# An opening in long rows with products of zeros, and splits of weights moved behind nearer work, in a one-layer hybrid encoder kernel

## The reference

```python
h = rmsnorm(x, g_norm1); z = h @ w_in
rq, rk, rv, rg, fq, fk, fv, ff, mq, gl = jnp.split(z, SPLIT_POINTS, axis=-1)
mk, mv = jnp.split(rmsnorm(mem, g_mem_in) @ w_mem_kv, 2, axis=-1)   # 256 memory tokens
# o_r: retention; o_f: forgetting attention; o_m: attention into the memory tokens
merged = (gates[..., 0, :] * (o_r @ w_br_ret)
          + gates[..., 1, :] * (o_f @ w_br_fox)
          + gates[..., 2, :] * (o_m @ w_br_mem))
x = x + merged @ w_out
return x + hier_moe(rmsnorm(x, g_norm2), ...)   # top-1 of 4 groups, top-2 of 8 experts in it
```

## Time and profile before

| | us |
|---|---|
| median of 3 runs (lowest to highest) | 654.72 (654.51 to 655.26) |
| the profiled execution | 654.53 |
| its span, first to last instruction | 652.6 |
| PE busy in it | 630.6 |
| DVE busy | 341.8 |
| ACT busy | 255.9 |
| POOL busy | 126.8 |

### The profile page before, as it was taken

How to read it: one execution, slowest core, us unless ns; L and a number is a source line. 1 busy time by engine, 2 the same in 40 slices (tenths; PEclk the granted TensorE clock), 3 DMA queues, 4 the chain that set the end, 5 groups by cost and what they waited for, 6 DMA issues and landing times.

```text
span 652.6 us, 9424 instructions
## 1 busy us (share of the span) xinstructions
PE 630.6 (97%) x3509; PEld 422.7 (65%) x3509; DVE 341.8 (52%) x729; ACT 255.9 (39%) x489; POOL 126.8 (19%) x142
## 2 busy tenths in 40 slices
PE   5999999999999999999999999999999999999995
PEld 4888888877888776778777878764434444344431
DVE  4649347885456565754446855575433434334312
ACT  5673343336424555564953334332221212221200
POOL 0018525663000310010000010012301311210301
PEclk9999999999999999999999999999999999999999
DMA  8975432354212833203967989399999999999993
GB/s 307 421 278 193 152 128 101 113 211 169 97 66 97 298 130 130 98 33 130 341 214 294 428 321 372 138 411 351 428 424 425 427 427 425 425 427 426 426 420 122
DMA packets 36096, 176.67 MB, mean 271 GB/s; under 512 B 4256, under 2 KB 4528, under 8 KB 23632
## 3 DMA queue, kind: packets, MB, share of 16 engines
q1 hardware_dynamic: 33072, 164.87, 64.0%
q0 software_dynamic: 2976, 11.16, 4.8%
HBM read 167.48 MB, written 9.06 MB: 270 GB/s over the span
## 4 chain that ended last, share of the span: by engine, by line
PE 80%; SPq 5%; DMA 5%; ACT 5%; issue 2%; DVE 2%; POOLq 0%; ACTq 0%; POOL 0%; DVEq 0%
PE banks L1718 15%; PE banks L1720 15%; PE banks L1719 15%; PE banks L2101 12%; PE banks L2131 6%; SPq L835 5%; DMA piece<-in_wexp 4%; PE banks L2085 2%; PE banks L2141 1%; DMA raw<-in_wstream 1%; ACT z L1140 1%; PE banks L1926 1%; ACT w_hi L1020 1%; PE banks L2006 1%; PE banks L1892 1%
## 5 line engine op out<-in xcount | busy, mean ns | idle before, releaser
L1263 DVE TENSOR_TENSOR w_lo<-raw,w_hi 128x1024 fp32r<-128x1024 f32 (+1 forms) x81 | 125.0, 1554 | 75.0 <-ACT w_hi L1020 74.8
L1718 PE MATMUL banks<-w_hi,hT_hi 128*128 128x512 f32 x312 | 124.6, 399 | 1.0 <-ACT z L1047 0.9
L1720 PE MATMUL banks<-w_hi,hT_lo 128*128 128x512 f32 x312 | 122.0, 391 | 0.0
L1719 PE MATMUL banks<-w_lo,hT_hi 128*128 128x512 f32 x312 | 121.7, 390 | 0.0
L1020 ACT ACTIVATE w_hi<-raw 128x1024 fp32r<-128x1024 f32 x79 | 83.5, 1057 | 90.1 <-PE banks L1720 86.1
L2101 PE MATMUL banks<-piece,xs 128*64 128x512 f32 x512 | 114.7, 593 | 0.5 <-DMA piece<-in_wexp 0.5
L2101 PEld LDWEIGHTS banks<-piece,xs 128*64 128x64 f32 x512 | 38.5, 137 | 72.6 <-issue 70.1
L1718 PEld LDWEIGHTS banks<-w_hi,hT_hi 128*128 128x128 f32 x312 | 58.7, 188 | 13.5 <-issue 2.1
L1720 PEld LDWEIGHTS banks<-w_hi,hT_lo 128*128 128x128 f32 x312 | 58.6, 188 | 12.6
L1719 PEld LDWEIGHTS banks<-w_lo,hT_hi 128*128 128x128 f32 x312 | 58.8, 188 | 11.3
L2131 PE MATMUL banks<-piece,act_T 128*64 128x512 f32 x256 | 58.5, 599 | 0.1
(11 more groups left out here) (358 smaller groups left out, 949.9 us busy)
## 6 DMA issues: line engine op xcount, KB each, us to landing
piece<-in_wexp SPq DMA_DIRECT2D x90, 1024.0 KB, 18.5
raw<-in_wstream SPq DMA_DIRECT2D x79, 512.0 KB, 4.6
piece<-in_wexp SPq DMA_DIRECT2D x12, 512.0 KB, 20.6
foxc<-in_foxc POOLq DMA_DIRECT2D x8, 512.0 KB, 4.9
memv<-in_memc SPq DMA_DIRECT2D x8, 512.0 KB, 4.9
memk<-in_memc SPq DMA_DIRECT2D x8, 512.0 KB, 5.1
xT<-in_xT SPq DMA_DIRECT2D x1, 1536.0 KB, 11.5
xtok<-in_xtok SPq DMA_DIRECT2D x1, 1536.0 KB, 7.9
```

The lines of the kernel that those rows point to most:

```text
L1263: dve.tensor_tensor(w_lo[:, i % PART_SLOTS, cols], raw[:, i % RAW_SLOTS, cols], w_hi[:, i % PART_SLOTS, cols].bitcast(F32), ALU.subtract). ...
L1718: mm(out, xh, wh, start=start, stop=False, skip_group_check=True)
L1719: mm(out, xh, wl, start=False, stop=False, skip_group_check=True)
L1720: return mm(out, xl, wh, start=False, stop=stop, skip_group_check=True)
```

## The change

- **Opening.** The gains of the first two norms and the first half of the transposed memory are packed on the host into one array `opening` (rows of 1040 floats), loaded in one transfer. Granule 0 comes whole, then granule 1, then the rest of the memory, then granules 2 and 3. `xT` follows granule 5 instead of granule 3, and `prep_x` moves from behind granules 1 to 3 to behind granules 4 to 6. `gk` keeps only the gain of the last norm and is loaded at granule 4. Granule 1, like 0, is split in halves.
- **Products of zeros.** Before its first step PE does 26 products of 128x256 of a tile that POOL sets to zero at the start, into bank 7, which nothing reads. Of granule 0 the first two products (high by high) wait only for the high parts.
- **Splits.** The split of 13 moves ahead of the evacuations of chunks 0 and 1; those of 37 to 40 move behind the next group of turns (37 behind the evacuation of chunk 8 and five turns, 38 behind seven, 39 behind eight, 40 behind `decay_sums`); those of 63 and 65 move behind the merges of chunks 15 and 16. In those places `granule(g, 1)` leaves one split ahead in front of the granule, and `splits(n)` adds those up to n later.
- **Granules.** 51, with the evacuation of chunk 12, moves ahead of the transposes and softmax steps of the unit there. 66 and 67 move into the end of the attention, each cut in two slices. 73 is cut in two around `turn_merged 1`.
- **SP.** Pieces 0, 1 and 2 are loaded together when the attention is done; before, 0 was, and 1 and 2 followed at granules 66 and 67.

```diff
@@ schedule
-    prep = {1: [("prep_x", k) for k in range(3)], 2: [("prep_x", k) for k in range(3, 6)], 3: [("prep_x", 6), ("prep_x", 7), ("prep_ff",)], 9: [("norm1",)]}
+    prep = {4: [("prep_x", k) for k in range(3)], 5: [("prep_x", k) for k in range(3, 6)], 6: [("prep_x", 6), ("prep_x", 7), ("prep_ff",)], 9: [("norm1",)]}
...
+    def granule(g, ahead=ahead):
+        splits(g + 1 + ahead)
         s.append(("k", g))
         s.extend(prep.get(g, []))
...
-            granule(g)
+            granule(g, 1 if g == FIRST[C_GATE] - 1 else ahead)
             if g == FIRST[C_RQK] + 2:
+                s.append(("split", split))
+                split += 1
                 s += [("evac", C_MK), ("post", C_MK), ("evac", C_MV), ("post", C_MV)]
...
         if i in (4, 11, 19):
-            gate()
+            gate(1)
...
         opened(i)
+        if j == 3:
+            gate()
         turned(i - 2, True)
...
-    granule(r + 1)
+    granule(r + 1, 1)
     merge(r + 1)
+    splits(r + 4)
...
-    granule(r + 3)
+    granule(r + 3, 1)
     merge(r + 3)
+    splits(r + 6)
...
-    s += [("unit_o", n + 1), ("unit_p", n + 2), ("unit_v", n + 2), ("unit_p", n + 3), ("unit_o", n + 2), ("unit_v", n + 3), ("unit_o", n + 3)]
-    s += [("attention_done",)] + [("parts", j) for j in range(8, 12)]
+    s += [("unit_o", n + 1), ("unit_p", n + 2)]
+    granule(r + 6)
+    s += [("unit_v", n + 2), ("unit_p", n + 3), ("k2", r + 6), ("unit_o", n + 2), ("unit_v", n + 3)]
+    granule(r + 7)
+    s += [("unit_o", n + 3), ("attention_done",), ("k2", r + 7)] + [("parts", j) for j in range(8, 12)]
     c = C_BR + 4
-    granule(FIRST[c] - 2)
-    granule(FIRST[c] - 1)
...
-    s.append(("turn_merged", 1))
+    s += [("turn_merged", 1), ("k2", a + 1)]
@@ SP
-            load(gk, io["gk"], s_memT[0])
-            load(memT[:, 0:2, :], io["memT"][:, 0:2, :], s_memT[0])
-            load(raw[:, 0, 0:512], io["wstream"][0, :, 0:512], raw_in[0])
-            load(raw[:, 0, 512:1024], io["wstream"][0, :, 512:1024], second_half_in)
-            load(memT[:, 2:8, :], io["memT"][:, 2:8, :], s_memT[1])
-            for g in range(1, RAW_SLOTS):
+            load(opening[:, 0:2 * KT + KT // 2 * NMEM], io["opening"], s_memT[0])
+            granule(0)
+            granule(1)
+            load(memT[:, 4:8, :], io["memT"], s_memT[1])
+            for g in range(2, RAW_SLOTS):
                 granule(g)
-            load(xT[:, :, :], io["xT"], s_xT_ffw)
-            load(ffw, io["ffw"], s_xT_ffw)
@@ PE
+            pe.wait_ge(zeros_and_new, 1)
+            for _ in range(26):
+                mm(ps[:, 7, 0:256], nf_p[:, 0:P], nf_p[:, :], start=True, stop=True, skip_group_check=True)
...
+                    if i == 0:
+                        pe.wait_ge(act_hi, 2)
+                        pe.wait_ge(hi_ready, 1)
+                        for t in range(nt):
+                            mm(ps[:, bank_of(0, t), :], memT_hi[:, 0, t * P:t * P + P], w_hi[:, 0, 0:512], start=True, stop=False, skip_group_check=True)
```

More of the change, by code:

```diff
@@ L91, in schedule, with splits @@
     split = ahead + 1
-    prep = {1: [("prep_x", k) for k in range(3)], 2: [("prep_x", k) for k in range(3, 6)], 3: [("prep_x", 6), ("prep_x", 7), ("prep_ff",)], 9: [("norm1",)]}
-    def granule(g):
+    prep = {4: [("prep_x", k) for k in range(3)], 5: [("prep_x", k) for k in range(3, 6)], 6: [("prep_x", 6), ("prep_x", 7), ("prep_ff",)], 9: [("norm1",)]}
+    def splits(n):
         nonlocal split
-        while split < min(g + 1 + ahead, NGRAN):
+        while split < min(n, NGRAN):
             s.append(("split", split))
             split += 1
+    def granule(g, ahead=ahead):
+        splits(g + 1 + ahead)
         s.append(("k", g))
@@ L123, in schedule, with gate @@
     gates = iter(range(FIRST[C_GATE], FIRST[C_BR]))
-    def gate(evacs=s):
+    def gate(ahead=ahead):
         g = next(gates)
-        granule(g)
+        granule(g, ahead)
         if g + 1 in FIRST:
-            evacs.append(("evac", chunk_at[g]))
+            s.append(("evac", chunk_at[g]))
     chunk_at = [c for c in range(len(CHUNKS)) for _ in range(FIRST[c], FIRST[c + 1])]
@@ L400, in program @@
         ident = cst("ident")
[L401 removed]
+        gk = sm(KT)
         ss, rstd = sm(5), sm(5)
@@ L922, in _ @@
                     sp.wait_ge(br_add, 3)
-                    load_piece(0)
+                    for c in range(3):
+                        load_piece(c)
                 elif kind == "residual" and i == 0:
@@ L1016, in _ @@
                         act.activation(w_hi[:, 0, 0:512], raw[:, 0, 0:512], ACT.Copy).then_inc(hi_ready, 1)
-                        act.wait_ge(second_half_in, 16)
                         act.activation(w_hi[:, 0, 512:1024], raw[:, 0, 512:1024], ACT.Copy).then_inc(hi_ready, 1)
+                    elif i == 1:
+                        for half in range(2):
+                            cols = slice(512 * half, 512 * half + 512)
+                            act.activation(w_hi[:, 1, cols], raw[:, 1, cols], ACT.Copy).then_inc(hi_ready, 1)
                     else:
@@ L1259, in _ @@
                         dve.wait_ge(gran_used, i - PART_SLOTS + 1)
-                    for half in range(2) if i == 0 else (None,):
-                        dve.wait_ge(hi_ready, 1 if half == 0 else i + 2)
+                    for half in range(2) if i < 2 else (None,):
+                        dve.wait_ge(hi_ready, low_of(i) - (half == 0))
                         cols = slice(0, 1024) if half is None else slice(512 * half, 512 * half + 512)
@@ L1774, in _ @@
                             w = i % PART_SLOTS
-                            ins = parts(acc, xh[:, j, tok], xl[:, j, tok], w_hi[:, w, cols], w_lo[:, w, cols], first, last)
+                            if i == 0 and kk == 0:
+                                mm(acc, xh[:, j, tok], w_lo[:, w, cols], start=False, stop=False, skip_group_check=True)
+                                ins = mm(acc, xl[:, j, tok], w_hi[:, w, cols], start=False, stop=last, skip_group_check=True)
+                            else:
+                                ins = parts(acc, xh[:, j, tok], xl[:, j, tok], w_hi[:, w, cols], w_lo[:, w, cols], first, last)
                             if what == "out" and last and t < 2:
@@ L2276 @@
     arrays = {
-        "xT": turned(x), "xtok": by_token(x, T), "memT": turned(mem), "memtok": by_token(mem, 2), "gk": c(gk), "gain": c(np.tile(gain, (P, 1))),
+        "xT": turned(x), "xtok": by_token(x, T), "memT": c(memT[:, 4:]), "memtok": by_token(mem, 2), "gk": c(by_feature[2]),
+        "opening": c(np.concatenate(by_feature[:2] + [memT[:, :4].reshape(P, -1)], axis=1)), "gain": c(np.tile(gain, (P, 1))),
         "const": const, "const2": const2, "dtab": dtab, "qtab": qtab, "ffw": c(wff.reshape(KT, P, 8).transpose(1, 0, 2).reshape(P, 64)),
```

66 lines of the change are left out of this document (37 added, 29 removed).

## The result

| us | before | after |
|---|---|---|
| median of four runs (lowest to highest) | 654.65 (654.51 to 655.26) | 649.36 (648.57 to 649.76) |
| the profiled execution | 654.53 | 649.76 |
| its span | 652.6 | 648.0 |

The ratio is 0.9916, 95% interval 0.9904 to 0.9928: 5.3 us faster, where 5.4 was forecast (649.3). One thing to keep in mind: the profiled execution of the changed kernel is the slowest of the four.

A forecast was written before the change was run, and what follows sets the result against it. The end of the dense part starts PE and the piece stream together, so gains before granule 79 move the end. 1.8 + 0.7 + 0.35 + 0.45 + 1.3 + 0.85 = 5.45 us won, forecast 649.3 us, range 646.8 to 652.2.

The forecast's parts named there:

- The two rivals that rested on the stream of pieces: Expert part: the stream holds the end at 654.7 (chance 0.07); or PE waits for a piece, clock falls, 656.9 (0.04).
- Opening: Start of the kernel: 1.8 us won, bounds -0.3 and 2.3, with granule 3 at 16.4 against 18.29.
- the transfers cost a part of it: Opening: 0.26 MB more cost 0.78 us, less 0.40 for `gk`, so ACT begins granule 0 at 6.9, not 6.54.
- the gain comes from the clock: Opening: products of zeros raise the clock at 5.5, so products of weights start 0.23 us apart instead of 0.44.
- the clock is not won: Opening: zeros do not raise the clock earlier, or it falls, or granule 0 lands later; 650.8; chance 0.20.
- The idle 1.5 us: Opening: PE idles from the end of the products of zeros at 6.2 until the first real product at 7.7.
- The bound from granule 9's landing: Opening: granule 9 is split only from 31.18, when its data lands, so no more than 2.3 us can be kept.
- Turns 0.7: Six-fold transposes: splits moved behind the turns take away most of a 0.87 us stall; 0.7 won, bounds 0 and 1.0.
- granule 51 0.35: Granule 51 with the evacuation of chunk 12: transposes lie in front during ACT's copies; 0.35 us won, bounds 0 and 0.9.
- merges: Merges of chunks 15 and 16: 0.45 us won, bounds 0 and 1.9; the rest is waited for at `pT`.
- 73: Granule 73 around `turn_merged 1`: the 0.66 us stall before granule 74 goes; 0.85 won, bounds 0 and 1.0.
- Attention's end 1.3: Granules 66 and 67 in the end of the attention: their slices fill PE's gaps; 1.3 us won, bounds 0 and 1.7.

The follow-up runs named there:

- numbers 1: The changed kernel run again with no edit: 648.99 us (648.25 to 651.70), ratio 0.992.
- 7: The changed kernel with granules 66 and 67 put behind the attention again: 649.08 us.
- Number 8: The changed kernel with granule 65 also cut in two slices around transposes, and the values step in front of granule 66: 647.81 us, ratio 0.9897.
- Number 2: The changed kernel without the 26 products of zeros: 649.38 us (649.10 to 649.62).
- 3: The changed kernel with the load of `xtok`, `gain` and `gk` one step later, behind granule 9: 648.01 us, ratio 0.9896.
- 4: The changed kernel with `xtok` loaded behind granule 9 and no products of zeros: 649.24 us.
- Number 5: The kernel before with the 26 products of zeros alone: 654.95 us, ratio 1.0011; run once more, 656.33 us, ratio 1.0019.
- 11: The changed kernel with `xtok` loaded behind granule 9 and 14 products of zeros instead of 26: 648.99 us.
- number 10: The changed kernel with `xtok` behind granule 9, the edit of Number 8, and the split of 65 behind the transposes of unit 32: 646.62 us, ratio 0.9875.

## Why the prediction was right, and where its steps were not

**What bounds the kernel: right.** The end of granule 79, the first piece and the end of the span moved by 4.60, 4.60 and 4.69. In every run from the end of granule 79 to the end of the span it was 236.8 to 237.4 us. The two rivals that rested on the stream of pieces found nothing.

**The total: partly luck.** The stages behind the opening gave 3.2 where 3.65 was forecast: 1.0 too little at the attention's end, 0.6 more than forecast elsewhere. The opening, forecast at 1.8, gave 1.4 in the first profile and 2.3 to 3.0 in those of numbers 1, 7 and 8. That these came to 5.3 against 5.4 in the medians of four executions is not to the credit of the sum.

**Opening: the size was 1.8, the runs give 1.4 to 3.0; two of its steps failed.** The first was "the transfers cost a part of it". They gained. The 0.26 MB more did not move granule 0's split from 6.54 to 6.9; it started at 5.82 in the first profile, and at 5.4 to 5.5 in those of numbers 1 to 4. Granule 1, split from 10.27 before, is split from 8.06. The issue view shows it, before and after:

```profile
memT<-in_memT SPq DMA_DIRECT2D x1, 256.0 KB, 3.9
```

```profile
opening<-in_opening SPq DMA_DIRECT2D x1, 520.0 KB, 3.3
```

Twice the bytes landed 0.6 us sooner after their issue, and 1.05 us earlier in the span (by ACT's first rows, 4.08 against 5.13). The windows of 1 us show when the data began to flow:

```profile
1.00:2.00 1.00, 0.00 (x0) 0.00 (x0) 0.00 (x0) 1.00 (x1) 0.04 (x1) 1.00 0.10 12
2.00:3.00 1.00, 0.00 (x0) 0.00 (x0) 0.00 (x0) 0.01 (x1) 0.00 (x0) 1.00 0.35 111
3.00:4.00 1.00, 0.00 (x0) 0.00 (x0) 0.00 (x0) 0.00 (x0) 0.00 (x0) 1.00 0.74 225
4.00:5.00 1.00, 0.00 (x0) 0.00 (x0) 0.00 (x0) 0.00 (x0) 0.00 (x0) 1.00 1.05 283
```

```profile
1.00:2.00 1.00, 0.90 (x4) 0.90 (x5) 0.00 (x0) 1.00 (x1) 0.04 (x1) 1.00 0.30 62
2.00:3.00 1.00, 1.00 (x7) 1.00 (x7) 0.00 (x0) 0.02 (x1) 0.00 (x0) 1.00 0.86 320
3.00:4.00 1.00, 1.00 (x6) 1.00 (x6) 0.00 (x0) 0.00 (x0) 0.00 (x0) 1.00 1.00 383
4.00:5.00 1.00, 1.00 (x7) 1.00 (x6) 0.37 (x1) 0.91 (x2) 0.00 (x0) 1.00 1.33 340
```

From 1 to 5 us this is 0.63 MB before and 1.11 MB now. My 330 GB/s were of a window in which the stream was running; before, it started late. I counted bytes at a steady rate where the cost was in getting going. Whether it was the small rows of `gk`, the number of transfers or the length of their rows was not tried apart. The Trainium skill, "DMA: Bandwidth & Descriptors", section "Anatomy of one DMA — SWDGE (gpsimd) path", would have said 2.0 + 0.53 MB at 436 GB/s = 3.2 us for `opening`; the trace has 3.3, though SP issued it. I set that aside because the first piece before took 3.9 where it gives 2.6, but that was the second transfer of a queue, and `opening` is the first. By that fit the prediction had `opening` and granule 0 there at about 5.6, nearer to the 5.4 to 5.8 of the runs than my 6.9. The handoff to PE, which I had put at 0.15 without a row, was 0.15 in the first profile (5.82 + 0.63 to 6.60).

The second was "the gain comes from the clock". Number 5 has the clock without the transfers: nothing. Number 2 has the transfers without the zeros: 1.9 of the 2.6 us at granule 10. Both together are needed for the whole. In the kernel before, the landing of granule 1 covered the slow products; once it lands earlier, they are the bound, and only then are zeros worth something (1.2 to 1.6). For the same reason the rival "the clock is not won" had its price wrong: without any zeros the kernel took 649.38, not 650.8. The idle 1.5 us between the zeros and the first product of weights did not come about: the zeros ran up to it, at 6.60.

The bound from granule 9's landing (2.3 at most) was the right place to look: in the first profile it cut 2.40 to 1.39, and wherever PE waited there, the first product came 2.5 us after ACT began the split (32.05 and 34.58, 30.72 and 33.26, 31.13 and 33.66). But I took 31.18 for a constant, though the change moves `xT` behind two granules, and ACT's start varied between 30.4 and 32.1. In three of the five profiles with this opening more than 2.3 was kept at granule 9 (2.5 to 3.0).

**Turns 0.7, granule 51 0.35, merges 0.45, 73 0.85: right in mechanism**, measured 0.77, 0.52, 0.68, 0.95. The merges went as described: 1.49 was won at granule 62, and at granule 65 0.65 of it was left, the rest waited for at `pT`. The turns' two thirds and the 0.35 for granule 51 were guesses between bounds, and came within 0.2. The 0.45 was low by 0.2: the second wait, with its hidden part, was 0.4 where I had 0.35, and `pT` came 0.1 sooner than by the shift; the last 0.1 I did not trace.

**Attention's end 1.3: wrong by 1.** I counted the stalls that go (1.6) and took off 0.3 for the merge. The merge alone cost 0.63, the parts of the attention output before granule 68 0.30, and each of four more changes from transposes to products some 0.1, which appears as a first product of 0.47 to 0.50 instead of 0.39. What I failed to ask was what the first filler itself waits for: granule 66 writes the banks that the merge in front of it reads, at the same moment as `pT` is awaited. The stall before got a new owner and kept its length (0.68, then 0.63, with the hidden parts). Number 8 removed it: the second slice of granule 65, which needs neither, covers `pT`, and the values step covers the merge.

**The range** (646.8 to 652.2) held all runs of the four; the repeated kernel's too.

## What to carry to other kernels

A cost in front of a wait is free until the wait goes, so an edit on each of two things that hide one another measures as nothing, and both together as the whole; try them in pairs before dropping one. A filler is only worth its place if what it waits for is ready there: look up its banks' last reader as well as its inputs. And a bound that is taken from a transfer's landing holds only as long as the order of transfers in front of it stays; if the change moves one, work the landing out anew, and expect the spread from run to run to show there.

## What the runs showed of the hardware

- By the spacing of the products (0.43 us, then 0.23; products of zeros 0.21, then 0.12) the clock rose 3.9 to 4.4 us after the first product of weights in numbers 2, 4 and 11 and the kernel before. With 26 products of zeros in front it rose 3.4 us after the first of them in both profiles of number 5, 4.0 in number 10's, and 5.0 to 5.6 in the others. In number 5 it held through an idle time of 2.5 us: the products behind it are 0.23 apart. The Trainium skill, "TensorE: Matmul & The Clock Gate", section "Part 1: The HAM clock gate (the "warmup" mystery)", says that the moment varies from run to run. The profiles agree: the first profile and number 10's have the same opening, and the clock rose 5.1 and 4.0 us after the first product.
- The windows' clock column reads 1.00 from 6 to 10 us in number 2, where products are 0.43 apart. In an opening the spacing of the products tells the clock, not the column.
